# Moving the state-space input stage ahead of the memory attention, and interleaving a gemm with the output stage

## The reference, cut to what matters

```python
u, z, xq = split_cols(h @ w_in, [SEQ_WIDTH, MIX_WIDTH, XA_WIDTH])        # 2048, 3072, 1024
# per group of 16 channels: x_t = Ab x_{t-1} + Bb u_t (64 complex states), y_t = Re(C x_t)
y = s5_chunked(uf.reshape(b_, l_, S5_GROUPS, S5_GROUP), ab_re, ab_im, bb_re, bb_im, c_re, c_im)
y = y.reshape(b_, l_, SEQ_WIDTH) + d * uf
y = jax.nn.gelu(y)
y = y * jax.nn.sigmoid(y @ w_glu + b_glu)
xa = memory_attention(xq, mem_n, xa_w_kv[i])
y = jnp.concatenate([y, xa], axis=-1) * jax.nn.silu(z)
x = x + y @ w_out[i]
```

## Time and profile before

| | us |
|---|---|
| median of 3 runs | 4038.22 (4034.9 to 4045.0) |
| profiled execution | 4035.01, span 4033.4 |
| TensorE busy | 3347.7 (83% of the span) |
| VectorE, ScalarE, GpSimd busy | 1380.2, 858.9, 941.7 |
| mean granted TensorE clock | 0.868 |

### The profile page before, as it was taken

One profiled execution on the slowest core, in us unless ns is written; L12 is line 12 of the kernel. 1 busy time (PEld: TensorE's weight loads), 2 busy tenths in 40 slices (PEclk: granted clock), 3 DMA queues, 4 the chain that ended last, 5 costly groups with the idle time before them and its releaser, 6 DMA issues.

```text
span 4033.4 us, 43394 instructions
## 1 busy us (share of the span) xinstructions
PE 3347.7 (83%) x16218; PEld 2493.2 (62%) x16218; DVE 1380.2 (34%) x2299; ACT 858.9 (21%) x1401; POOL 941.7 (23%) x658
## 2 busy tenths in 40 slices
PE   7997976698987967798986787799998955679998
PEld 4444744476665457344775686689997733337776
DVE  5662023401012630003144653360513153446052
ACT  2112222123121101201234211131222122222221
POOL 0321400243122035002431000033432310003443
PEclk9998976799987965899987996899999965589999
DMA  5991200023356347121220000122221200012222
GB/s 166 255 265 38 94 16 0 32 94 115 125 84 178 99 125 211 58 76 64 94 77 32 1 1 1 42 76 81 89 84 65 73 0 0 0 42 84 89 89 78
DMA packets 112552, 322.25 MB, mean 80 GB/s; under 512 B 35472, under 2 KB 36112, under 8 KB 112160
## 3 DMA queue, kind: packets, MB, share of 16 engines
q1 hardware_dynamic: 59040, 212.89, 15.6%
q0 software_dynamic: 31168, 95.17, 9.1%
q10 hardware_dynamic: 22208, 12.26, 1.1%
HBM read 288.38 MB, written 31.85 MB: 79 GB/s over the span
## 4 chain that ended last, share of the span: by engine, by line
PE 73%; DVE 15%; issue 4%; ACT 3%; POOL 2%; DMA 2%; DVEq 0%; ACTq 0%; POOLq 0%
PE ps L229 15%; PE ps L221 12%; PE ps L224 12%; PE ps L226 11%; DVE inv L461 2%; PE ps L1881 2%; DVE h L469 2%; POOL ring_r L347 1%; PE ps L251 1%; PE ps L449 1%; PE ps L1910 1%; PE ps L245 1%; PE ps L249 1%; PE ps L248 1%; DMA arena<-d_pb 1%
## 5 line engine op out<-in xcount | busy, mean ns | idle before, releaser
L347 POOL TENSOR_TENSOR ring_r<-ring,high 128x1024 fp32r<-128x1024 f32 x274 | 700.7, 2557 | 2116.9 <-ACT high L265 2116.9
L221 PE MATMUL ps<-h_hi,high 128*128 128x264 f32 (+1 forms) x1632 | 516.9, 329 | 62.6 <-DVE h_r L474 41.1
L224 PE MATMUL ps<-h_r,high 128*128 128x264 f32 (+1 forms) x1632 | 512.2, 327 | 0.0
L226 PE MATMUL ps<-h_hi,ring_r 128*128 128x264 f32 (+1 forms) x1632 | 444.8, 325 | 0.0
L265 ACT ACTIVATE high<-ring 128x1024 fp32r<-128x1024 f32 x274 | 289.0, 1055 | 544.9 <-PE ps L221 420.4
L229 PE MATMUL ps<-arena,ring 128*128 128x512 f32 (+1 forms) x896 | 337.2, 539 | 51.6 <-ACT arena L1212 36.1
L221 PEld LDWEIGHTS ps<-h_hi,high 128*128 128x128 f32 x1632 | 311.5, 191 | 100.7 <-issue 59.5
L229 PE MATMUL ps<-h,ring 128*128 128x512 f32 x768 | 331.8, 594 | 3.8 <-ACT arena L2206 2.3
L224 PEld LDWEIGHTS ps<-h_r,high 128*128 128x128 f32 x1632 | 313.3, 192 | 24.2
L229 PEld LDWEIGHTS ps<-arena,ring 128*128 128x128 f32 x896 | 172.3, 193 | 216.0 <-issue 154.1
L226 PEld LDWEIGHTS ps<-h_hi,ring_r 128*128 128x128 f32 x1632 | 275.8, 191 | 25.5
(11 more groups left out here) (379 smaller groups left out, 4920.8 us busy)
## 6 DMA issues: line engine op xcount, KB each, us to landing
ring<-in_units SPq DMA_DIRECT2D x402, 512.0 KB, 3.2
arena<-d_ca POOLq DMA_DIRECT2D x32, 640.0 KB, 4.7
d_ca<-arena POOLq DMA_DIRECT2D x16, 640.0 KB, 5.1
arena<-in_s_bk POOLq DMA_DIRECT2D x16, 512.0 KB, 9.4
arena<-d_q POOLq DMA_DIRECT2D x32, 256.0 KB, 11.4
d_pb<-arena POOLq DMA_DIRECT2D x16, 512.0 KB, 6.3
arena<-d_pb POOLq DMA_DIRECT2D x16, 512.0 KB, 5.5
arena<-d_k POOLq DMA_DIRECT2D x128, 64.0 KB, 4.5
```

What stands on the lines that cost most here:

```text
L221: part = mm(acc, hi[:, cols], self.x_hi(k)[:, t0:t0 + tn], start=(k == 0), stop=False)
L224: mm(acc, hi[:, cols], self.x(k)[:, t0:t0 + tn], start=False, stop=False)
L226: ins = mm(acc, w[:, cols], self.x_hi(k)[:, t0:t0 + tn], start=False, stop=(k == self.kt - 1))
L347: b.nc.gpsimd.tensor_tensor(b.ring_r[:, slot, :], b.ring[:, slot, :], self.high[:, j % 2, :], ALU.subtract).then_inc(b.unit_lo, 1)
```

## The change

- S5Inputs and S5Scan come right after mem_k1, ahead of mem_v1, xq1 and z1_xa. u is loaded to another place, which is later overwritten, so GpSimd also saves it to DRAM (`d_rows`, 4 MB, one DMA) after the tables of blocks 0 and 1.
- `state` is laid out as [group, step]; the scan has 63 steps. Its coefficients and products stay where they were.
- xa1 also waits for the scan.
- Rejoin is gone; z1 becomes a split gemm and is no longer a stage of its own on TensorE, ScalarE and GpSimd: S5Outputs issues one output tile of it ahead of each of its own blocks (`beside`). Its loops are written out.
- S5Outputs loads the 128 columns that it needs of `ca`, and per block the rows of u from `d_rows`. It uses banks 4 and 5.
- mem_v1's and xq1's outputs are copied by ScalarE alone.
- glu waits for each gelu by itself, at its first output.

```diff
@@ Gemm
+    def out_tensor(self, pe, n):
+        it, o = divmod(n, self.body_outs)
+        self.one_out(o, it)
+    def out_scalar(self, act, n):
...
+            self.make_high(act, 0, 0)
+        for u in range(n * units, n * units + units):
+            if u + 1 < total:
+                it, j = divmod(u + 1, self.body_units)
+                self.make_high(act, j, it)
...
+        act.wait_ge(b.filled[par], full)
+        self.store("act", n, self.bank(o), o).then_inc(b.stored[par], 1)
+    def out_gpsimd(self, pool, n):
+        if n == 0:
+            self.make_low(pool, 0, 0)
...
+                self.make_low(pool, j, it)
@@ S5Inputs.gpsimd
         load(0, 0)
         load(1, 1)
+        pool.wait_ge(self.u_in, 16 * S5_C)
+        pool.dma_start(b.d_rows, m.u.rearrange("p g j -> p (g j)")).then_inc(self.u_saved, 16)
@@ S5Inputs.vector
-            to = m.state[:, 1:S5_J + 1, bass.ds(m_ * 8, 8)].rearrange("p j g -> p g j")
+            to = m.state[:, bass.ds(m_ * 8, 8), 1:S5_J]
@@ S5Scan.vector
-        with dve.Fori(0, S5_J) as j:
-            old, new = m.state[:, j, :], m.state[:, j + 1, :]
-            tt(m.t1, b.a8[:, 0, :], old, ALU.mult).then_inc(self.step, 1)
+        re, im, t1, t2 = b.a8[:, 0, :], b.a8[:, 1, :], b.p[:, 0, 0:P], b.p[:, 1, 0:P]
+        with dve.Fori(0, S5_J - 1) as j:
+            old, new = m.state[:, :, j], m.state[:, :, j + 1]
+            tt(t1, re, old, ALU.mult).then_inc(self.step, 1)
...
@@ S5Outputs.gpsimd
+        load_tables(0)
+        load_tables(1)
+        for n in range(NB):
+            self.beside.out_gpsimd(pool, n)
+            if n == 0:
...
+                load_rows(0)
+                load_rows(1)
+            if n >= 2:
+                fetch(n - 2)
+            pool.wait_ge(self.mixed, n + 1)
+            if n + 2 < NB:
+                load_tables(n + 2)
+                load_rows(n + 2)
@@ S5Outputs.tensor
+        for n in range(NB):
+            par = n % 2
+            self.beside.out_tensor(pe, n)
+            pe.wait_ge(self.block_in[par], (n // 2 + 1) * 16 * self.LOADS)
...
+                mm(to, m.toep[par][:, g, :], m.rows[par][:, g, :], start=True, stop=False)
+                ins = mm(to, m.ca_out[par][:, g, :], m.state[:, n * 8 + g, :], start=False, stop=True)
@@ S5Outputs.scalar
+        for n in range(NB):
+            par = n % 2
+            self.beside.out_scalar(act, n)
+            act.wait_ge(self.mixed, n + 1)
...
+        for n in range(NB):
+            act.wait_ge(self.skipped, n + 1)
+            f(m.y[:, n, :], m.y[:, n, :], ACT.Gelu_apprx_tanh).then_inc(self.gelued, 1)
@@ build
+        s5i = S5Inputs(b, m5, u_all, tables.done, km_done)
+        stages.append(s5i)
+        scan = S5Scan(b, m5, [s5i.done])
+        stages.append(scan)
+        stages.append(Gemm(b, "mem_v1", "tm", memn, KD, 2, None, tm_keep(vm1), A, [(s5i.u_saved, 16), (s5i.k_kept, NB)], MEM_TILES))
...
-        stages.append(Rejoin())
...
+                              [(b.stored[0], g.done[0]), (b.stored[1], g.done[1]), scan.done])
...
-        gz = Gemm(b, "z1", "fm", h1, KD, NB, FULL,
+        gz = Gemm(b, "z1", "fm", h1_lo, KD, NB, FULL,
                   lambda which, m, parts, o: nc.scalar.activation(m0.z[:, m, :], parts[0], ACT.Silu), A,
-                  [(s5i.x_kept, NB), (s5i.k_kept, NB), (rejoined, KD)])
+                  [], high=high, x_hi=h_hi)
...
-                       bias=b.cols[:, bass.ds(m + col_at("s5_b_glu"), 1)]), A, [s5o.done],
+                       bias=b.cols[:, bass.ds(m + col_at("s5_b_glu"), 1)]), A, [(b.stored[0], gz.done[0]), (b.stored[1], gz.done[1])],
+                   ready=s5o.tile,
```

More of the change, by code:

```diff
@@ L119, in __init__ @@
         self.squared_by = None
+        self.beside = False
         self.after = after
@@ L211, in feature_major @@
             for o in range(self.body_outs):
[L212 to L227, removed]
@@ new lines, in feature_major, with one_out @@
+                one_out(o, it)
+        def one_out(o, it):
+            free(o, it)
+            for c in range(self.per_out):
+                w = self.unit(pe, it, o * self.per_out + c)
+                for k in range(8 * c, 8 * c + 8):
+                    if self.high is not None:
+                        if self.ready and o == 0 and isinstance(it, int) and it == 0:
+                            pe.wait_ge(*self.ready(k))
+                        cols, hi = slice(k % 8 * P, (k % 8 + 1) * P), self.high[:, (o * self.per_out + c) % 2, :]
@@ L292, in scalar @@
     def scalar(self, act):
+        if self.beside:
+            return
         if self.high is None:
@@ L486, with __init__ @@
 class MemoryAttention(Stage):
[L490 removed]
+    def __init__(self, b, name, q, k, v, z, pt, needs):
+        self.pt = pt
         self.b, self.q, self.k, self.v, self.z, self.needs = b, q, k, v, z, needs
@@ L1025, in tensor @@
         b, m, mm = self.b, self.m, self.b.nc.tensor.matmul
-        for s, v in self.needs:
+        for s, v in self.banks_free:
             pe.wait_ge(s, v)
@@ L1070, in vector @@
         b, m, v = self.b, self.m, self.b.nc.vector
-        for s, n in self.needs:
+        for s, n in self.sent:
             dve.wait_ge(s, n)
@@ L1090, in __init__ @@
         self.step = b.sem("s5s_step")
-        self.done = (self.step, 5 * S5_J)
+        self.done = (self.step, 5 * (S5_J - 1))
     def vector(self, dve):
@@ L1128, in __init__ @@
         self.gelued = b.sem("s5o_gelued")
-        self.done = (self.gelued, NB)
-    loop = S5Inputs.loop
+        self.tile = lambda k: (self.gelued, k + 1)
+    LOADS = S5_C + 2
     def gpsimd(self, pool):
@@ L1214, in scalar @@
-        self.loop(act, block)
-        with act.Fori(0, NB) as i:
-            gelu(i)
+        for n in range(NB):
+            act.wait_ge(self.skipped, n + 1)
+            f(m.y[:, n, :], m.y[:, n, :], ACT.Gelu_apprx_tanh).then_inc(self.gelued, 1)
     def vector(self, dve):
         b, m = self.b, self.m
-        def skip(m_, par, n):
-            dve.wait_ge(self.back[par], n)
-            y = m.y[:, m_, :]
-            b.nc.vector.scalar_tensor_tensor(out=y, in0=m.ustage[par], scalar=b.cols[:, bass.ds(m_ + col_at("s5_d"), 1)],
-                                             in1=y, op0=ALU.mult, op1=ALU.add).then_inc(self.skipped, 1)
@@ L1226, in vector @@
-        with dve.Fori(0, NB // 2) as it:
-            for par in range(2):
-                skip(it * 2 + par, par, it * 32 + 32)
+        for n in range(NB):
+            dve.wait_ge(self.back[n % 2], (n // 2 + 1) * 32)
+            y = m.y[:, n, :]
+            b.nc.vector.scalar_tensor_tensor(out=y, in0=m.ustage[n % 2], scalar=b.col("s5_d", n), in1=y, op0=ALU.mult,
+                                             op1=ALU.add).then_inc(self.skipped, 1)
 RW_PAIRS = 4
@@ L2387, in build @@
[L2387 to L2395 removed]
+        gz = Gemm(b, "z1", "fm", h1_lo, KD, NB, FULL,
+                  lambda which, m, parts, o: nc.scalar.activation(m0.z[:, m, :], parts[0], ACT.Silu), A, [],
+                  high=high, x_hi=h_hi)
@@ L2396, in build @@
         stages.append(gz)
-        stages.append(S5Scan(b, m5, [s5i.done]))
-        s5o = S5Outputs(b, m5, [(b.stored[0], gz.done[0]), (b.stored[1], gz.done[1]), stages[-1].done, (s5i.added, NB), (s5i.k_stored[0], 8 * NB), (s5i.k_stored[1], 8 * NB)])
+        s5o = S5Outputs(b, m5, gz, [scan.done, (s5i.added, NB), (s5i.k_stored[0], 8 * NB), (s5i.k_stored[1], 8 * NB)],
+                        [att.done])
         stages.append(s5o)
```

208 lines of the change are left out of this document (99 added, 109 removed).

## The result

The changed kernel took **3996.6 us** (median of 4 runs, 3989.2 to 4003.0) against 4036.9 for the kernel before (median of 4), a ratio of **0.9897, 95% interval 0.9876 to 0.9918**: faster by some 40 us. The forecast was 4022 with a range of 3984 to 4064, so the sign and the range held, and the forecast was 25 us too slow.

A forecast was written before the change was run, and what follows sets the result against it. The prediction took the scan on VectorE to bound the old order and the new one. Its terms put glu's first output at 1637.3 against 1653.7, -16.4 us, giving 4018.6 profiled and 4022 us as median, range 3984 to 4064.

The forecast's parts named there:

- (a): Between the last store of u and S5Inputs: added wait for u's loads, costing TensorE 43.8 us.
- (b): S5Inputs: 97.5 us from its first matmul as before, with block 2 coming 9 us later behind the store of u.
- (c): Scan on VectorE: strided state makes a step 2.52 us, GpSimd's subtractions hold it for 38.4 us; 197.2 us in all.
- (d): Attention xa1: 56.3 us plus 1.7 for a first score that Rejoin used to cover.
- (e): z1 outputs between S5Outputs blocks: first block 15.6 us, then 15 periods of 10.4, 171.6 us in all.
- (f): Tail after the last block: one table load for 16 gelus, last gelu ending 16.2 us later; glu's first output at 1637.3.
- The bound of 2.01, strides free: Scan: a step stays at 2.01 us if strided access costs nothing, sum falls by 32 us; as a rival, chance 0.16.
- Rival 2: Interleaved loop of z1 and S5Outputs: clock falls in every block, period 12.8 us, +36 us, 4058; chance 0.26.
- Rival 3: Interleaved loop: DMA engines set the pace, period 11.4 us, +15 us, 4037, no change; chance 0.17.

## Why the prediction was right in sign and 25 us too slow

Lengths in us, predicted and measured in the profile:

| step | predicted | measured | error |
|---|---|---|---|
| (a) last store of u to S5Inputs | 73.3 | 72.9 | -0.4 |
| (b) S5Inputs | 106.5 | 107.4 | +0.9 |
| (c) scan | 197.2 | 192.7 | -4.5 |
| (d) xa1 | 58.0 | 59.3 | +1.3 |
| (e) z1 and blocks | 171.6 | 153.4 | -18.2 |
| (f) tail | 17.0 | 22.9 | +5.9 |
| stretch | 623.6 | 608.6 | -15.0 |

**(a)** The terms hold. The wait was 20.4 us in front of S5Inputs and 18.4 inside mem_k1, whose weights shared the full DMA engines; I had put it as one wait of 43.8. The load took about 68 us (1004.3 to 1072.1), 65 predicted.

**(b)** The length is right and its reason is not. I let the store of u hold block 2 back by 9 us; by the start of block 2 it was 2 to 4. What made up the rest of the 10 us over the old 97.5 is open: the clock was 0.71 against 0.80, but nearly the same code took anything from 97.7 to 107.7 us. That the sum came out within a microsecond is luck.

**(c)** Both halves are shown, each by its own run: the stride +0.51 us a step, as I had it, and 16 holds (I had 16 x 2.4 = 38.4; 16 operations of 39.7 us in all, less the 0.4 each would take, is 33 to 34). That I priced the hold too high is nearly all of the 4.5 us. (My +0.51 should have been 3 x 0.08 + 2 x 0.13 = 0.50, and the upper bound 2.65, not 2.68.) The bound of 2.01, strides free, falls: the Trainium skill (VectorE: DVE Perf Modes, Mode 1x) says that odd strides work in the fallback mode at one result a cycle, and here operations at a stride of 256 bytes took 0.37 to 0.45 us where contiguous values took 0.29. That they work is true; that they are free is not.

**(d)** holds.

**(e) is the step that failed.** "Three resources lie within 0.6 us. The old loop ran at 142.6/16 = 8.9 against 7.1 of TensorE, a factor of 1.25; [...] so I take 10.4, between 9.6 and 1.25 x 9.6 = 12.0." I carried an allowance for waiting over from a loop with little slack between a transfer's issue and its use. Here there is a whole gemm output in between, and the loop ran almost without waiting: no wait for a transfer, 1.4 us for GpSimd, and all three resources at 0.91 to 1.00. The bare blocks of the run with z1 apart did wait for transfers, 21.8 us. The floor itself was too high as well: 9.6 of TensorE was 9.11, since a block took 3.5 us between outputs, not 4.0. In the error of 18.2 us, the 15 periods are 17.1 (156.0 predicted, 138.9 measured) and the first block 1.0; of the 1.3 us by which the usual period is shorter, 0.8 was the allowance and 0.5 the floor. The clock was 0.99, as the forecast had it. Rival 2's premise is true for bare blocks, at 0.50 with z1 apart, and false for interleaved ones: the dense 5.6 us in each period decided it.

**(f)** The last gelu ended 14.1 us after the last block's copy began, sooner than the 16.2 I had, but glu's first output came 8.7 us after that; I had counted 0.8. That output is 32 passes, two a gelu. They began with the first gelu, at 1593.9, and took 0.5 us each at a mean clock of 0.78, while a gelu came every 0.53. So TensorE set the end and not the gelus. My own rows could have told it: two passes of 0.44 are longer than a gelu of 0.63.

Rival 3 (engines set the pace at 11.4) is out: they sustained a share of 1.00 at a period of 9.11.

The whole: 16.4 predicted, 31.6 in the stretch, about 40 by the medians. Of the 8 us between the last two, the shift of the first layer in this profile is one example of what can move them; the interval of the ratio, 33 to 50 us faster, begins just above the 31.6.

## What to carry to other kernels

When a serial stage is moved, price it in its new company: here the reordering left VectorE's scan as the bound, and its two new costs (a stride, and an engine that holds it) made 62 us of idle TensorE, which two free PSUM banks cut to 25. An interleaved loop can run, as this one nearly did, at the sum of its fullest engine with nothing on top, when each transfer has a whole other stage's work to arrive in; take an old loop's waiting factor only where the slack is the same. A load whose source is written piece by piece should be issued piece by piece.

## What the runs showed of the hardware that was not expected

- Moving one input of every operation of the scan to PSUM took away the whole hold (16 of 315 operations at 2.40 to 2.54 us, then none, at the same GpSimd work) and shortened the undisturbed step as well, by 0.10 us.
- The DMA engines held a share of 1.00 to 1.04 at 279 to 287 GB/s in the loop, but the load of u, in runs of 256 bytes on the DRAM side, kept them at 0.96 to 0.99 for 129 to 149 GB/s, weights included: full engines are no measure of bytes.
- Unchanged code moves. S5Inputs, from its first matmul to the scan's first operation, took 97.7 to 107.7 us over the eleven profiles of the new order (in three of them its transfers came in another order), at mean clocks of 0.68 to 0.83, and not in the order of the clock. The length of such a stage in a single profile can't show an effect under some 10 us; the start of one block can.
